# ScalarE copies the value stage's finished PSUM banks to SBUF, VectorE adds from there, with ten coefficient slots in place of eleven

## What is computed

```
q = (xb @ w_q).reshape(PEER_BLOCK, PEER_HEADS, 2, PEER_DQ // 2)
scores = jnp.einsum('bhsd,hskd->bhsk', q, sub_keys).astype(jnp.float32)
...
top_v, top_pos = lax.top_k(cand, PEER_TOPK)
eidx = jnp.take_along_axis(cidx, top_pos, axis=-1)
gate = jax.nn.softmax(top_v, axis=-1)
act = jax.nn.gelu(jnp.einsum('bhkd,bd->bhk', u_sel, xb))
v_sel = jnp.take(v_tab, eidx, axis=0)
return jnp.einsum('bhk,bhkd->bd', gate * act, v_sel)
```

## Time and profile before

| | |
|---|---|
| median of 3 runs | 5185.88 us |
| lowest, highest | 5175.16, 5192.61 us |
| the profiled execution | 5189.77 us, its span 5188.0 us |
| mean granted TensorE clock | 0.954 |
| TensorE busy over the span | 4836.2 us (93%) |
| VectorE, ScalarE, GpSimd busy | 2422.8, 985.9, 632.2 us |
| value stage: first and last start of line 2050 | 3897.7 and 5142.0 us |
| matmuls of lines 2050 to 2052 | 3 x 2048 |
| line 1556 | 240 adds of 546 ns median, 16 copies of 549 ns |
| DMA over the span | 155 GB/s mean; 319 to 346 GB/s in most slices of the value stage |

### The profile page before, as it was taken

The page is one execution under the profiler, slowest core; times in us unless marked ns, Lnnn a source line. Parts: engine busy times, 40 slices in busy tenths (PEclk is TensorE's granted clock), DMA queues, the critical chain, the costliest instruction groups (busy, mean ns, idle before and its releaser), DMA issues.

```text
span 5188.0 us, 68670 instructions
## 1 busy us (share of the span) xinstructions
PE 4836.2 (93%) x29440; PEld 4222.8 (81%) x29440; DVE 2422.8 (47%) x3614; ACT 985.9 (19%) x1117; POOL 632.2 (12%) x446
## 2 busy tenths in 40 slices
PE   8899999999968969999999999999998888898898
PEld 4577778755524539999999999999998888898897
DVE  0378221012251032266777761111114887888886
ACT  1000101000020011122223441111212222222222
POOL 0000000000000000000000000000006885333320
PEclk9999999988889989999999999999999999999999
DMA  6311111144441112133333443333336999989984
GB/s 251 101 66 50 70 67 54 65 147 147 143 154 73 65 69 73 68 105 106 111 107 118 163 158 110 104 104 104 108 130 197 339 319 346 338 327 343 341 320 151
DMA packets 233885, 805.61 MB, mean 155 GB/s; under 512 B 48736, under 2 KB 127744, under 8 KB 177744
## 3 DMA queue, kind: packets, MB, share of 16 engines
q1 hardware_dynamic: 178688, 534.78, 30.1%
q0 software_dynamic: 34832, 204.94, 10.6%
q10 hardware_dynamic: 20160, 62.92, 3.0%
HBM read 724.74 MB, written 77.84 MB: 155 GB/s over the span
## 4 chain that ended last, share of the span: by engine, by line
PE 81%; DMA 8%; POOL 5%; DVE 3%; issue 2%; ACT 1%; SPq 0%; DVEq 0%; ACTq 0%; POOLq 0%
PE PS L1972 12%; PE PS L1974 12%; PE PS L1973 12%; PE PS L1837 11%; PE PS L1648 6%; PE PS L1952 5%; DMA arena<-in_peer_v 4%; PE PS L1840 4%; POOL attw L648 4%; PE PS L2050 4%; PE PS L2051 4%; PE PS L2052 4%; PE PS L2024 2%; DMA out_n_s<-arena 2%; POOL arena L656 1%
## 5 line engine op out<-in xcount | busy, mean ns | idle before, releaser
L1972 PE MATMUL PS<-h_hi,blk_hi 128*128 128x288 f32 x4608 | 1368.2, 297 | 58.3 <-DVE blk_lo L1408 53.8
L1974 PE MATMUL PS<-h_hi,blk_lo 128*128 128x288 f32 x4608 | 1358.9, 295 | 0.0
L1973 PE MATMUL PS<-h_lo,blk_hi 128*128 128x288 f32 x4608 | 1358.7, 295 | 0.0
L1972 PEld LDWEIGHTS PS<-h_hi,blk_hi 128*128 128x128 f32 x4608 | 866.3, 188 | 59.2 <-issue 50.9
L1973 PEld LDWEIGHTS PS<-h_lo,blk_hi 128*128 128x128 f32 x4608 | 866.4, 188 | 0.0
L1974 PEld LDWEIGHTS PS<-h_hi,blk_lo 128*128 128x128 f32 x4608 | 865.8, 188 | 0.0
L2050 PE MATMUL PS<-co_hi,ev_hi 128*128 128x384 f32 x2048 | 701.0, 342 | 142.1 <-DVE arena L1556 140.9
L1408 DVE TENSOR_TENSOR blk_lo<-arena,blk_hi 128x2048 fp32r<-128x2048 f32 x144 | 329.9, 2291 | 820.4 <-ACT blk_hi L871 819.9
L2051 PE MATMUL PS<-co_lo,ev_hi 128*128 128x384 f32 x2048 | 697.7, 341 | 0.0
L2052 PE MATMUL PS<-co_hi,ev_lo 128*128 128x384 f32 x2048 | 696.8, 340 | 0.0
L1837 PE MATMUL PS<-arena 128*128 128x288 f32 x2176 | 549.2, 413 | 2.2 <-ACT arena L725 2.2
(11 more groups left out here) (400 smaller groups left out, 4243.2 us busy)
## 6 DMA issues: line engine op xcount, KB each, us to landing
arena<-in_peer_ut SPq DMA_DIRECT2D x128, 1024.0 KB, 5.4
arena<-in_peer_v SPq DMA_DIRECT2D x256, 512.0 KB, 7.1
arena<-in_w_ada SPq DMA_DIRECT2D x48, 2048.0 KB, 7.9
activation_scratch<-arena ACTq DMA_DIRECT2D x128, 288.0 KB, 5.5
arena<-in_w_f SPq DMA_DIRECT2D x17, 2048.0 KB, 7.7
gate_scratch<-arena ACTq DMA_DIRECT2D x12, 2048.0 KB, 7.2
arena<-activation_scratch SPq DMA_DIRECT2D x32, 768.0 KB, 11.9
arena<-gate_scratch SPq DMA_DIRECT2D x32, 768.0 KB, 15.5
```

The lines of the kernel that those rows point to most:

```text
L1972: mm(split(k)[:, x], hi[:, c], h_part[0][:, c, cols], start=c == 0, stop=False)
L1973: mm(split(k)[:, x], hi[:, c], h_part[1][:, c, cols], start=False, stop=False)
L1974: ins = mm(split(k)[:, x], lo[:, c], h_part[0][:, c, cols], start=False, stop=c == KC - 1)
```

## The change

- After `value_high(8m + 2)` and the coefficient copy that may stand there, ScalarE copies the eight finished banks of round m - 1 to SBUF (`sums_out`, new), in four buffers of 384 columns (`part_sum`, `SUMS` = 4). It waits for `vp_made` or `ev_made` as VectorE did, and from the fifth copy on for the add of the copy four before it. It increments `ps_out`.
- VectorE's `add_half` stands where it was, waits for `ps_out` and adds from `part_sum`.
- TensorE waits for `ps_out` where it waited for `acc_made`, in the rounds and at the end.
- The four buffers take the SBUF space of one coefficient slot (two parts of 384 columns) and a further 768 columns' room: `COS` is 10, and the places of some buffers move. `co_step` gives one unit later for every block from 8 on, with which the coefficients' multiplication and conversion and the factor loads come one unit later.

```
-RAWS, HIS, COS, ROWS = 6, 4, 11, 5
+RAWS, HIS, COS, ROWS, SUMS = 6, 4, 10, 5, 4
...
-        RAW_AT = [41088 + 1024 * k for k in range(3)] + [26624 + 1024 * k for k in range(3)]
-        HI_AT = [44160, 45184, 29696, 30720]
+        RAW_AT = [41088 + 1024 * k for k in range(3)] + [25856 + 1024 * k for k in range(3)]
+        HI_AT = [44160, 45184, 28928, 29952]
...
+        part_sum = [at(30976 + TD * k, TD) for k in range(SUMS)]
...
-            return 2 * RND * (n // RND) - RND + 1 + n % RND
+            return 2 * RND * (n // RND) - RND + 2 + n % RND
...
+            def sums_out(m):
+
+                for c in range(RND):
+                    j = RND * m + c
+                    if c < RND - 1:
+                        act.wait_ge(vp_made, (RND - 1) * m + c + 1)
+                    else:
+                        act.wait_ge(ev_made, RND * (m + 1))
+                    if j >= SUMS:
+                        act.wait_ge(acc_made, j - SUMS + 1)
+                    act.activation(part_sum[j % SUMS], bank((c + 6) % 8, 0, TD), ACT.Copy).then_inc(ps_out, 1)
+
...
+                if k % RND == 2 and k > RND:
+                    sums_out(k // RND - 1)
+            sums_out(UNITS // RND - 1)
...
             def add_half(m):
 
                 for c in range(RND):
-                    if c < RND - 1:
-                        dve.wait_ge(vp_made, (RND - 1) * m + c + 1)
-                    else:
-                        dve.wait_ge(ev_made, RND * (m + 1))
-                    dst, src = acc[:, RND * (m % 2) + c], bank((c + 6) % 8, 0, TD)
+                    j = RND * m + c
+                    dve.wait_ge(ps_out, j + 1)
+                    dst, src = acc[:, RND * (m % 2) + c], part_sum[j % SUMS]
                     ins = dve.tensor_copy(dst, src) if m < 2 else tt(dst, dst, src, ALU.add)
                     ins.then_inc(acc_made, 1)
...
                     if m and i == 0:
-                        pe.wait_ge(acc_made, RND * (m - 1) + c + 1)
+                        pe.wait_ge(ps_out, RND * (m - 1) + c + 1)
...
-            pe.wait_ge(acc_made, 2 * NK)
+            pe.wait_ge(ps_out, 2 * NK)
```

2 lines of the change are left out of this document (1 added, 1 removed).

## The result

The changed kernel has a median of 5198.02 us (5190.28 to 5209.79, 17 runs), the kernel before beside it 5184.43 us (17 runs): **ratio 1.0033, 95% interval 1.0024 to 1.0042**, some 14 us slower. The forecast was 5185 us and no change. The range held the time, but the likeliest case, no change, did not come true.

A forecast was written before the change was run, and what follows sets the result against it. GpSimd was taken to set the pace before unit 96, then late-landing loads plus 6.3 us from landing to TensorE's start. Terms + 8 - 3 - 6 + 0.5, about -1 us, gave 5185 us, range 5155 to 5208 us.

The forecast's parts named there:

- + 8 (adds): Before unit 96, adds with two SBUF inputs hold up GpSimd's gathers: 8 us lost, between 5 and 11.5.
- - 3 (TensorE nearer): Before unit 96, TensorE starts rounds earlier and comes closer to VectorE, once, at unit 88: 3 us gained.
- - 6 (boundaries): At eight late round boundaries after unit 96, 3.3 us gained less 2.6 lost, 0.7 each: 6 us gained.
- + 0.5: At the end of the stage, the last add follows its copy: 0.5 us lost.
- The added copies: ScalarE's 256 copies out of PSUM take 0.5 us each, covered by TensorE's later need: cost nothing.
- TensorE's wait moves to the copy: At a late boundary TensorE starts 3.3 us earlier if the load of unit 114 lands where it did.
- The shift of the loads: Factor loads one unit later make load 114 land 2.6 us later a boundary, bounds 0 and 4.2.
- The slot fewer: One coefficient slot fewer moves conversions and factor loads one unit later, priced as load 114's later landing, 2.6 us.
- C: Rival, chance 0.08: the second factor pair meets gathered rows and delays load 118, 2 us at eight boundaries: 5201 us.
- D: Rival, chance 0.11: ScalarE's fifth copy waits for VectorE's first add, so all gains are gone: 5194 us.
- B: Rival, chance 0.14: GpSimd is held for whole runs of adds before unit 96, 31 us lost, not 8: 5208 us.
- A: Rival, chance 0.25: load 114's landing doesn't move, 3.3 us gained at each of nine boundaries: 5161 us.

The follow-up runs named there:

- e3: The kernel before with its adds reading a fixed SBUF buffer instead of PSUM, the dense sum left out of the result; ratio 1.0028.
- e1: The changed kernel with each pair of factor loads issued one unit earlier, where the kernel before had it; ratio 1.0022.
- e4: e1 with ScalarE's copies only from round 11 on, VectorE adding from PSUM until then; ratio 0.9982.
- e5: The changed kernel with ScalarE's copies only from round 11 on, VectorE adding from PSUM until then; ratio 1.0023.
- e12: The kernel before with the adds from round 11 on placed behind unit 8m+1's low part instead of unit 8m+2's; ratio 0.9910.
- e8: e4 run again on another chip; ratio 0.9988.
- e9: The changed kernel with copies from round 11 on, two copy buffers and eleven coefficient slots, coefficient steps and loads as in the kernel before; ratio 0.9960.
- e10: e5 with copies and adds from round 11 on placed behind unit 8m+1 instead of unit 8m+2; ratio 0.9949.
- e13: The changed kernel with copies and adds placed behind unit 8m+1 instead of unit 8m+2 in all rounds; ratio 0.9977.
- e6: The kernel before with the factor pairs issued from ScalarE's queue instead of between SyncE's value loads; ratio 1.0012.

## Why the prediction was wrong

The sum was + 8 (adds) - 3 (TensorE nearer) - 6 (boundaries) + 0.5. **Two of its steps failed**, and the total, 14 us over, needs both:

- up to unit 96 a loss of 5 (8 less 3) was forecast. The result's traces have 9, those of the second chip 31. The term that was mis-sized most is that of the adds;
- from unit 96 on a gain of 6 was forecast. The result's traces have a loss of 2, because the moved loads land later than was put in.

Term by term:

- **The adds read two SBUF tiles, + 8 us**, bounds 5 and 11.5. In the result's traces it can't be more than the 9 us. On other chips, measured in medians: 15 us (e3, interval 5 to 23), 18 (e1 less e4), 18 (changed less e5; these two take the copies of the early rounds away too). Each of the three is uncertain by about 10 us, but they agree, and the gathers point the same way. Only the gathers that begin under adds were counted, 33 of them; there were 26, and they cost 4.3 us directly. The durations of all 256 gathers up to the 64th row sum to 373.8 us against 363.2, and the 64th row is issued 11 us later, counted from the first gather, where 8 was forecast. The rest of the difference lies under row steps (4.0), low parts (2.3) and co_lo (1.4), with 1.1 less under the products of activations and gates: a gather that ends later meets the next VectorE instruction otherwise. On the chips of e1, e3 and the two further traces of the changed kernel there are 12 to 17 us of gathers held over several instructions on top, which no step of the prediction has. In all traces the sum is 371 to 382 us with SBUF adds and 350 to 372 without, and 7 to 26 us apart within a chip. How the rest of the loss splits between the gathers and what follows from the fuller VectorE stays open. The Trainium skill's "SBUF — State Buffer", section "Who interferes with whom", which the prediction weighed, pointed the right way.
- **What bounds the kernel.** Right for the early stretch: GpSimd's time and the stage's time grew together in every pair of a chip, though not one for one. Too narrow for the late one. It read the wait as late landing plus 6.3 us of hand-over and listed the very instructions ahead of the add, but took their order as given. e12 shows what the order was worth: 47 of 89 us of waiting, half directly and half through loads that landed earlier.
- **The added copies**: cost nothing, as far as the runs show. e3 has a loss of this size without them.
- **TensorE's wait moves to the copy**: a gain of 3.3 us a boundary was forecast. At the eight boundaries 112 to 224 the hand-over from the high part of 8m+2 falls from 4.8 us to 1.6, 3.2 less: right. With the loads back (e1, e4, e8) the late stretch is 674.3 to 683.4 us against 693.5 to 706.4, some 20 us in ten boundaries, 2 each.
- **The shift of the loads**: 2.6 us a boundary was forecast. The high part of 8m+2 comes 8.7 us after the round's end on average (7.5 forecast) and came 5.0 after it before: 3.7 us, so that gain and loss cancel and nothing is left of the 6 us. The late stretch is 699 us against 697 where 691 was forecast; over all traces it is 690 to 699 against 693 to 706, so a gain of a few us is not excluded. e5 less e8 is 10 us from unit 96 on, on one chip. Right in mechanism; the shift was put 1.1 us a boundary too small, 9 us in eight.
- **The slot fewer** was costed only through the loads. Giving it back together with the coefficient steps is worth 12 us (e8 to e9).
- **TensorE nearer to VectorE, - 3 us**: not there. At unit 88, for which it was reckoned, TensorE is held 4.0 us at bank 4, where it waited 2.4 us before the unit, and it goes on with matmuls of 0.52 us.
- **The rivals.** The prices of C and D (5201 and 5194) lie nearest to the 5198 us; B's, 22 us over the kernel before, is nearest on the two other chips, where it was some 29. None was right as a whole. D's mechanism holds up to unit 96: of 51.5 us that TensorE stands there at or in the first unit of a round, 41.6 are at bank 4 (the fifth chunk), whose copy waits for VectorE's first add. At the late even boundaries it isn't so: the first four copies go at once and TensorE isn't held. B's mechanism exists too: no gather that began under adds was held longer than 1.30 us, but one that began just ahead of a run was held over all of it, once before unit 96 in e1 and e3 each, never there in the result's trace. C is real but masked: its load 118 holds up nothing while the boundary wait stands, and costs 6 to 11 us in most even rounds once that is gone (e10, e13). A falls, the landing moved.

## What to carry to other kernels

When an engine's wait ends with an instruction of another, read what stands ahead of that one in the other's program and whether the waiting engine needs it. Here it was worth 44 us to move eight adds ahead of one conversion that TensorE didn't need yet, while handing the banks over by another engine, with the loads moved as a price, was worth nothing. An operand moved from PSUM to SBUF was not free on an engine that shares SBUF with a busy GpSimd: price every instruction of GpSimd in the stretch, not only those beside the changed one. Look also at what an edit of an experiment puts in the way itself: e6 took a load from behind two others and put its own issues ahead of ScalarE's work.

## What the runs showed of the hardware

- A gather of GpSimd that began under adds with two SBUF inputs ended 0.82 us after the end of the add under way, after 1.09 to 1.30 us in all; under adds with one PSUM input it took 0.95 us.
- A gather that began just ahead of back-to-back VectorE instructions with two SBUF inputs could be held over many of them, at most 6.84 us (e1, e3), and again ended 0.82 us after the end of one of them. Over a whole run of eight adds this came only with SBUF adds, eight times in the result's trace, and in no trace with PSUM adds throughout. When a gather gets in between two instructions and when not stays open.
- Late, 331 to 334 GB/s at a share of 0.91 looked like a bound and was none: with the adds in their earlier place the same stretch ran at 357 to 362 GB/s.
- In e6 from unit 96 on a pair of DMA issues on ScalarE took 1.0 to 1.3 us at one place in the period and 6 to 17 us at the other, and ScalarE's next instruction stood behind it.
- On the first three chips of the experiments TensorE stood idle 38 to 68 us in the first 24 units of the stage, between single matmuls, whichever kernel ran; on the other two and with the result it did not. What these matmuls waited for the traces don't say.
